# First two expert blocks selected by matrix products, and six blocks moved ahead of a program border

## The chip, the cores and the metric

The kernel runs on one core of a Trainium2 chip, in one launch. The metric is the device time of that core in microseconds (us). A lower time is better.

## The reference

Three transformer layers follow each other on 512 tokens of width 1024, all in float32. The first two have the same form: two kinds of attention, a mixture of experts, and a gated per-layer embedding. The third is of another kind and has no experts. The change touches only the mixture of experts:

```python
g_sel = jnp.argmax(g_logits, axis=-1)                       # one of 4 groups per token
e_prob = jax.nn.softmax(e_logits[rows, g_sel], axis=-1)
top_p, top_i = lax.top_k(e_prob, TOP_K)                     # 2 of the group's 8 experts
gates = g_p[:, None] * top_p / jnp.sum(top_p, axis=-1, keepdims=True)
expert_id = (g_sel[:, None] * EXPERTS_PER_GROUP + top_i).reshape(-1)
...
def expert_block(args):
    xb, e = args
    hid = jax.nn.silu(xb @ w_gate[e]) * (xb @ w_up[e])
    return hid @ w_down[e]
```

There are 32 experts. Each has a gate and an up matrix of 1024 x 256 and a down matrix of 256 x 1024, one megabyte each. Every token goes to two experts, and the two results are added to it with their weights.

## The kernel before, in words

Each of the first two layers has a routing block and an expert block, in the sense of a program block: the program of every engine is cut there, all engines wait for each other at the border, read a value, branch, and go on.

**Routing (`merge_and_route`, L1478).** After the output product of the attention, the tokens x lie in SBUF, 128 per tile in four tiles. TensorE turns x and multiplies it with the router's weights; VectorE finds the two experts of every token and writes `member`, a 0/1 table of tokens by experts. TensorE sums it (L1610, L1612), which gives each token its rank within its expert. From the ranks VectorE works out a slot for each of the 1024 pairs of token and expert, in blocks of 64 slots ("lanes"): block n holds the first 64 tokens of expert n. There are 32 of these, a 33rd for the first overflow, and a rare path (`spilled`) for more. TensorE turns the slots into the token table by L1620 and L1623: for each slot of each block, which token is in it. VectorE stores it as `r.token` and `r.row` (L1779 to L1783). ScalarE meanwhile writes the normed rows of x to DRAM (`xn_rows`, L1654 to L1661). GpSimd then gathers the rows of blocks 0 and 1 (L1561), one indirect transfer for a pair of blocks, into one of two tiles `xs`. This ends the routing block.

**Border.** L1484 waits for all engines, L3325 loads the number of overflow blocks into a register of each engine, and L3143 branches past the rare path.

**Experts (`experts`, L1843).** 33 blocks in order. TensorE's order for block n is: `gate_up(n)` (L1950, 16 products of 64 tokens with 256 columns, each two records in the trace); on even n the turning of the next pair's rows, `turn` (L1939); `down(n - 1)` (L1968); `turn_hidden(n)` (L1959). ScalarE does the silu and evicts the result of `down`; VectorE multiplies silu and up (L2021), copies the turned hidden tile (L2027), and scales the turned rows by the norm's gain (`xsT`, L2012). GpSimd scatters block n's result to DRAM (L1909) and gathers the pair after next (L1902).

**The weights.** Six slots hold the weights of six experts. The routing block's SyncE queue fills all six. In the expert block SyncE goes on with expert 6 in slot 0, and so on (L1885, L1887): gate and up of expert n wait until `gate_up(n - 6)` is done, its down matrix until `down(n - 6)` is done. All three are on one queue, in order:

```python
wait(sp, sem["gu_done"], n - U + 1)
for dst, src in (gate, up):
    sp.dma_start(dst, src).then_inc(w_landed[n % U], 16)
wait(sp, sem["down_done"], n - U + 1)
sp.dma_start(*down).then_inc(down_landed[n % U], 16)
```

The order of all of this is the order in which the code is written; no planner is at work.

Of the kernel before, what the change touches and what calls it, by code (L numbers as in the profile page):

```python
# [1476 lines left out]
def merge_and_route(k, tag, st, attention, second_ready, m, op, r, xn_rows, first, expert_loads, embedding, xs, gathered, done):  # L1477
# [6 lines left out]
    with ExitStack() as ctx:  # L1484
        def sb(name, shape, dt=F32):
# [5 lines left out]
        wide = sb("wide", [P, SPILL * NE])  # L1491
        lgT, ended = wide[:, 0:S // 2], wide[:].rearrange("p (s e) -> p s e", s=SPILL)
# [19 lines left out]
        lane_hot = sb("lane_hot", [P, 8, P], F32R)  # L1512
        block_token = sb("block_token", [P, 8, BLOCKS], F32R)
# [4 lines left out]
                 "gap_ready ratio_done member_ready ranked lane_hot_ready block_token_ready tabled halved cleared token_ready start_ready")  # L1518
        (link_sem, p_turned, gained_ready, turned, out_act, out_dve, logits_done, logits_out, logits_turned, gneg_ready, gexp_done,
         gap_ready, ratio_done, member_ready, ranked, lane_hot_ready, block_token_ready, tabled, halved, cleared, token_ready, start_ready) = sems(  # L1520
# [6 lines left out]
        def _(sp):  # L1527
# [17 lines left out]
            expert_loads.issue(sp, 10)  # L1545

        @block.gpsimd
        def _(pool):
            last_token = pool.to_reg(S - 1)
# [5 lines left out]
            for u in range(GATHERS):  # L1555
                nc.gpsimd.memset(xs[:, u, :], 0.0).then_inc(cleared, 1)
# [3 lines left out]
            for q in range(GATHERS):  # L1560
                nc.gpsimd.indirect_dma_start(out=xs[:, q, :], out_offset=None, in_=xn_rows[:, :],  # L1561
                                             in_offset=bass.IndirectOffsetOnAxis(ap=r.token[:, q:q + 1], axis=0),
                                             bounds_check=last_token, oob_is_err=False).then_inc(gathered[q], 16)

        @block.tensor
        def _(pe):
# [43 lines left out]
            nc.tensor.matmul(k.ps[:, 2, 0:NT * NE], k.neg_before[:], member[:], start=True, stop=False, skip_group_check=True)  # L1610
            for n in range(1, NT + 1):
                last = nc.tensor.matmul(k.ps[:, 2, n * NE:(NT + 1) * NE], k.neg_ones[:], member[:, 0:(NT + 1 - n) * NE],  # L1612
                                        start=False, stop=(n == NT), skip_group_check=True)
            last.then_inc(ranked, 1)

            pe.wait_ge(block_token_ready, 1)
            for i in range(8):
                if i % 4 == 0:
                    pe.wait_ge(lane_hot_ready, 1 + i // 4)
                last = nc.tensor.matmul(k.ps[:, 3, 0:BLOCKS], lane_hot[:, i, :], block_token[:, i, :], start=(i == 0), stop=(i == 7))  # L1620
# [224 lines left out]
def experts(k, ctx, room, tag, r, layer, first, blocks, xn_rows, y_rows, w_gate, w_up, w_down, xs, gathered, opening=None):  # L1845

    nc = k.nc
# [1609 lines left out]
```

## Time and profile before

| what | us |
|---|---|
| median of 3 runs (2473.07 to 2476.53) | 2473.22 |
| the profiled execution | 2474.32 |
| its span in the trace | 2472.4 |
| PE (TensorE) busy | 2280.0 (92%) |
| DVE (VectorE) busy | 993.5 (40%) |
| ACT (ScalarE) busy | 588.0 (24%) |
| POOL (GpSimd) busy | 402.7 (16%) |

402.86 MB go through the core's DMA queues, 372.56 MB of them on the hardware queue q1. The expert stage of the first layer lies at about 464 to 710 us of the span, that of the second at about 1235 to 1485 us.

How to read it: PE is the matmul part of TensorE and PEld its weight load, which runs beside it. A busy share is an average over stages with different limits, so what bounds the expert stage must be read there. "DMA share" is the mean busy share of the 16 DMA engines. A bracket at a row's end tells how long the engine was idle before it, and what ended that. A "q" after an engine's name means its sequencer. `PEclk` is the granted clock of TensorE, 1.00 for 2.4 GHz and 0.50 for 1.2 GHz.

### The profile page before, as it was taken

The numbers are of one execution on the slowest core, as the hardware profiler recorded it, in microseconds if no ns is written. First come the engines' busy times: TensorE is split into PE (matmuls) and PEld (weight loads), VectorE is DVE, ScalarE is ACT, GpSimd is POOL, SyncE is SP. The second block draws the span as 40 slices with busy tenths as digits, with TensorE's granted clock in tenths as the row PEclk, the third lists the DMA queues.
The fourth block names the chain that finished last, engine by engine and source line by source line (L and its number), as shares of the span: only waits on it lengthen the run. The fifth ranks groups of instructions, "written<-read, shape, count | busy, mean of one in ns | idle before, by whom it ended". The sixth has DMA issues, their size and how long they took to land. (4 is left out here: it accounts for less than half of the span.)

```text
span 2472.4 us, 29130 instructions
## 1 busy us (share of the span) xinstructions
PE 2280.0 (92%) x11792; PEld 1688.7 (68%) x11792; DVE 993.5 (40%) x1701; ACT 588.0 (24%) x1213; POOL 402.7 (16%) x399
## 2 busy tenths in 40 slices
PE   7989999689889989999698979899999999999998
PEld 6666788444447767788554446687767887888887
DVE  5545533311135444643411116455653334322234
ACT  3533301211123342410311113323441002100012
POOL 2011111112211101111111212111101211112111
PEclk9999999799989999999899999899999999999999
DMA  5114436699962202234789994332222333233321
GB/s 159 52 53 107 126 109 250 262 415 421 422 272 77 68 26 71 65 94 146 304 337 422 421 373 148 86 86 71 79 69 73 102 104 97 85 99 98 95 102 69
DMA packets 291897, 402.86 MB, mean 163 GB/s; under 512 B 31534, under 2 KB 230958, under 8 KB 273834
## 3 DMA queue, kind: packets, MB, share of 16 engines
q1 hardware_dynamic: 276000, 372.56, 42.1%
q0 software_dynamic: 10176, 16.81, 1.8%
q10 hardware_dynamic: 5578, 11.51, 1.7%
q8 instruction: 98, 1.61, 0.3%
q14 instruction: 45, 0.37, 0.0%
HBM read 388.98 MB, written 30.15 MB: 170 GB/s over the span
## 5 line engine op out<-in xcount | busy, mean ns | idle before, releaser
L138 PE MATMUL banks<-h_split,w_high 128*128 128x512 f32 x2624 | 825.7, 396 | 2.3 <-PEq L3142 1.7
L138 PEld LDWEIGHTS banks<-h_split,w_high 128*128 128x128 f32 x2624 | 480.9, 188 | 104.3 <-issue 8.2
L190 DVE TENSOR_TENSOR w_low<-w_raw,w_high 128x1024 fp32r<-128x1024 f32 (+1 forms) x264 | 316.8, 1201 | 502.3 <-POOL w_high L179 502.2
L179 POOL CAST w_high<-w_raw 128x1024 fp32r<-128x1024 f32 (+1 forms) x264 | 277.0, 1050 | 1458.9 <-PE banks L138 1334.1
L138 PE MATMUL banks<-h_split,w_low 128*128 128x512 f32 x1312 | 512.1, 390 | 0.0
L138 PEld LDWEIGHTS banks<-h_split,w_low 128*128 128x128 f32 x1312 | 246.2, 188 | 52.3
L138 PE MATMUL banks<-w_high,op_split 128*128 128x512 f32 x736 | 228.5, 390 | 1.4 <-DVE mg_part L1355 1.1
L1950 PE MATMUL banks<-expert_ring,ex_xsT 128*64 128x256 f32 x1472 | 181.6, 403 | 21.6 <-DMA expert_ring<-in_w_exp_up 18.6
L1950 PEld LDWEIGHTS banks<-expert_ring,ex_xsT 128*64 128x64 f32 x1472 | 108.0, 145 | 81.1 <-DMA expert_ring<-in_w_exp_up 20.5
L138 PEld LDWEIGHTS banks<-w_high,op_split 128*128 128x128 f32 x736 | 138.1, 188 | 31.9 <-DVE mg_part L1355 2.4
L138 PE MATMUL banks<-w_low,op_split 128*128 128x512 f32 x368 | 143.2, 389 | 0.0
L2021 DVE TENSOR_TENSOR ex_hid<-ex_silu,banks 128x128 f32<-128x128 f32 x66 | 19.0, 288 | 280.2 <-ACT ex_silu L1998 280.2
L1909 POOL DMA_INDIRECT y_rows<-ex_y,route_row x66 | 65.8, 997 | 388.2 <-ACT ex_y L1993 388.2
L138 PE MATMUL banks<-w_high,h_split 128*128 128x512 f32 (+1 forms) x384 | 120.2, 388 | 3.7 <-DVE h_split L361 3.5
L1339 ACT ACTIVATE mg_sig<-banks 128x512 f32<-128x512 f32 x44 | 26.4, 601 | 341.7 <-PE banks L138 341.7
L1968 PE MATMUL banks<-expert_ring,ex_hidT 128*64 128x512 f32 x368 | 90.8, 615 | 0.9 <-issue 0.9
L1939 PE MATMUL banks<-identity,ex_xs 128*128 128x128 f32 x272 | 41.4, 298 | 49.7 <-DMA ex_xs<-xn_rows,route_token 29.6
L138 PE MATMUL banks<-pg_high,h_split 128*128 128x512 f32 x256 | 84.4, 405 | 2.6 <-issue 2.6
L138 PEld LDWEIGHTS banks<-w_high,h_split 128*128 128x128 f32 x384 | 72.9, 195 | 18.6 <-DVE h_split L361 5.1
L1998 ACT ACTIVATE ex_silu<-banks 128x128 f32<-128x128 f32 x66 | 18.3, 278 | 271.7 <-PE banks L1950 271.7
L1950 PE MATMUL banks<-region,ex_xsT 128*64 128x256 f32 x640 | 75.2, 388 | 7.7 <-DMA region<-in_w_exp_up 7.7
L1993 ACT ACTIVATE ex_y<-banks 128x512 f32<-128x512 f32 x66 | 39.4, 597 | 170.7 <-PE banks L1968 170.7
(416 smaller groups left out, 2727.8 us busy)
## 6 DMA issues: line engine op xcount, KB each, us to landing
w_raw<-in_w_in SPq DMA_DIRECT2D x142, 512.0 KB, 4.0
expert_ring<-in_w_exp_gate SPq DMA_DIRECT2D x46, 1024.0 KB
expert_ring<-in_w_exp_up SPq DMA_DIRECT2D x46, 1024.0 KB
expert_ring<-in_w_exp_down SPq DMA_DIRECT2D x46, 1024.0 KB, 22.2
w_raw<-in_w_gu SPq DMA_DIRECT2D x44, 512.0 KB, 4.0
region<-in_w_exp_gate SPq DMA_DIRECT2D x20, 1024.0 KB
region<-in_w_exp_up SPq DMA_DIRECT2D x20, 1024.0 KB
region<-in_w_exp_down SPq DMA_DIRECT2D x20, 1024.0 KB, 17.6
```

The source lines that it names most:

```text
L138: last = nc.tensor.matmul(out, left, right, start=(start and n == 0), stop=(stop and n == 2), skip_group_check=True)
L179: self.nc.gpsimd.tensor_copy(self.high[:, i % self.SPLIT, 0:n], self.raw[:, i % self.RAW, 0:n]).then_inc(self.high_ready, 1)
L190: self.nc.vector.tensor_tensor(self.low[:, i % self.SPLIT, 0:n], self.raw[:, i % self.RAW, 0:n], self.high[:, i % self.SPLIT, 0:n].bitcast ...
L1339: self.nc.scalar.activation(out, gate, ACT.Sigmoid).then_inc(self.sig_done, 1)
L1909: nc.gpsimd.indirect_dma_start(out=y_halves, in_=y[:, n % Y, :], in_offset=None, out_offset=bass.IndirectOffsetOnAxis(ap=r.row[:, at:at + ...
L1939: last = nc.tensor.transpose(k.ps[:, c // 4, (c % 4) * P:(c % 4 + 1) * P], xs[:, q % X, c::DC], k.ident[:])
L1950: last = nc.tensor.matmul(k.ps[LANES * h:LANES * (h + 1), 2 + side, 0:2 * P].rearrange("p (g n) -> p g n", g=2), xsT[:, q % X, c, LANES * ...
L1968: last = nc.tensor.matmul(k.ps[LANES * h:LANES * (h + 1), 5 + n % 2, :], hidT[:, n % 2, LANES * f:LANES * (f + 1)], slots[n % U][1][:, f, ...
L1993: nc.scalar.activation(y[:, n % Y, :], k.ps[:, 5 + n % 2, :], ACT.Copy).then_inc(sem["y_ready"], 1)
L1998: nc.scalar.activation(silu[:, n % 2, :], k.ps[:, 2 + n % 2, 0:P], ACT.Silu).then_inc(sem["silu_done"], 1)
L2021: nc.vector.tensor_tensor(hid[:, n % 2, :], silu[:, n % 2, :], k.ps[:, 2 + n % 2, P:2 * P], ALU.mult).then_inc(sem["hid_ready"], 1)
```

## The change

**Blocks 0 and 1 without a gather.** For each of these two blocks VectorE makes a table `select` of tokens by 64 lanes from the ranks: the norm's factor where the token is in the lane, else 0. TensorE multiplies x with it (`pick`: 8 column groups by 4 tiles, 32 products with a 128x128 stationary tile of x and 64 moving columns). The result is the block's rows, already turned. ScalarE copies it with the gain (`take`, 8 copies of 128x64). `select` lies in the first `xs` tile.

**Six blocks in the routing block.** `gate_up`, `turn_hidden`, `down` and the rest of blocks 0 to 5 now stand in the routing block, before the border, and SyncE issues the loads of experts 6 to 11 there. The token table stands in front of block 0's products. After the border the expert block goes on with block 6. Its first step is to turn the rows of pair 3. The rare path moves to a function of its own, and restores slot 5 and the two gathered pairs.

```diff
+            def pick(b):
+                pe.wait_ge(select_ready, b + 1)
+                for c in range(DC):
+                    for t in range(NT):
+                        last = nc.tensor.matmul(e.pick(b, c), k.x[:, t, c::DC], select[:, b, t, :],
+                                                start=(t == 0), stop=(t == NT - 1))
+                    last.then_inc(e.selected, 1)
+
+            pe.wait_ge(p_taken, 1)
+            pick(0)
             pe.wait_ge(block_token_ready, 1)
...
             last.then_inc(halved, 1)
+            e.gate_up(pe, 0)
+            e.turn_hidden(pe, 0)
+            pick(1)
+            e.gate_up(pe, 1)
+            e.down(pe, 0)
+            e.turn_hidden(pe, 1)
+            e.turn(pe, 1)
+            pe.wait_ge(row_ready, 1)
+            e.down(pe, 1)
+            for n in range(2, EARLY):
+                e.gate_up(pe, n)
+                if n == 2:
+                    e.turn(pe, 2)
+                if n > 2:
+                    e.down(pe, n - 1)
+                e.turn_hidden(pe, n)
+            e.down(pe, EARLY - 1)
...
             expert_loads.issue(sp, 10)
+            for n in range(EXPERT_SLOTS, EXPERT_SLOTS + EARLY):
+                e.load(sp, n)
...
-            for q in range(GATHERS):
-                nc.gpsimd.indirect_dma_start(out=xs[:, q, :], out_offset=None, in_=xn_rows[:, :],
...
+            e.gather(pool, 1, last_token)
+            pool.wait_ge(e.selected, FIRST_PAIR * DC)
+            e.gather(pool, 2, last_token)
+            pool.wait_ge(row_ready, 1)
+            for n in range(EARLY):
+                if n and n % 2 == 0:
+                    pool.wait_ge(e.turned, n // 2)
+                    e.gather(pool, n // 2 + GATHERS, last_token)
+                e.scatter(pool, n, last_row)
...
+            def chosen(b):
+                link(V.tensor_tensor(select[:, b, :, :], lane_next[:].unsqueeze(1).to_broadcast([P, NT, LANES]),
+                                     next_rank[:, :, b:b + 1].to_broadcast([P, NT, LANES]), ALU.is_equal))
+                V.tensor_tensor(select[:, b, :, :], select[:, b, :, :], of_tile(norm.ss[:], LANES), ALU.mult).then_inc(select_ready, 1)
...
+EARLY = 6
...
+    def take(self, act, n):
+        for c in range(DC):
+            act.wait_ge(self.selected, n * DC + self.last_of_bank(n, c) + 1)
+            self.nc.scalar.activation(self.xsT[:, 0, c, LANES * n:LANES * (n + 1)], self.pick(n, c), ACT.Copy,
+                                      scale=self.r.gain[:, c:c + 1]).then_inc(self.taken, 1)
...
     def sync(sp):
-        for n in range(ahead, blocks):
...
+        for n in range(EXPERT_SLOTS + EARLY, e.blocks):
+            e.load(sp, n)
...
-    nc = bacc.Bacc("TRN2", target_bir_lowering=False, num_devices=1)
+    nc = bacc.Bacc("TRN2", target_bir_lowering=False, num_devices=1, dynamic_dma_scratch_size=4096)
```

The order of TensorE from the last rank products to the border, first layer, before:

```order
L1612 MATMUL banks<-rt_member,neg_ones 128x96
L1612 MATMUL banks<-rt_member,neg_ones 128x64
L1612 MATMUL banks<-rt_member,neg_ones 128x32
L1620 MATMUL banks<-rt_block_token,rt_lane_hot 128x48 x8
L1623 MATMUL banks<-rt_block_token,rt_lane_hot 128x48 x4
L1484 UNCONDITIONAL_BRANCH
L3325 TENSOR_LOAD route_spill_expert
L3143 COMPARE_AND_BRANCH
```

And changed (L1632 is `pick`, L2000 `gate_up`, L2009 `turn_hidden`, L2019 `down`, L1984 `turn`):

```order
L1624 MATMUL banks<-rt_member,neg_ones 128x32
L1632 MATMUL banks<-ex_xs,x_tokens 128x64 x32
L1642 MATMUL banks<-rt_block_token,rt_lane_hot 128x48 x8
L1645 MATMUL banks<-rt_block_token,rt_lane_hot 128x48 x4
L2000 MATMUL banks<-expert_ring,ex_xsT 64x256 x16
L2009 MATMUL banks<-identity,ex_hid 128x128
L1632 MATMUL banks<-ex_xs,x_tokens 128x64 x32
L2000 MATMUL banks<-expert_ring,ex_xsT 64x256 x16
L2019 MATMUL banks<-expert_ring,ex_hidT 64x512 x4
L2009 MATMUL banks<-identity,ex_hid 128x128
L1984 MATMUL banks<-identity,ex_xs 128x128 x8
L2019 MATMUL banks<-expert_ring,ex_hidT 64x512 x4
```

The table products (L1620, now L1642) stand behind the 32 products of block 0, and the expert products of six blocks stand before the border, of which the first ones are shown.

SyncE's queue at the same border, before and then changed (the last of the six loads in front of it):

```order
L121 DMA region<-in_w_exp_gate 128x2048
L121 DMA region<-in_w_exp_up 128x2048
L121 DMA region<-in_w_exp_down 128x2x1024
L1484 UNCONDITIONAL_BRANCH
L3325 TENSOR_LOAD route_spill_expert
```

These are the loads of the last slot filled ahead, slot 5. The same place in the changed kernel:

```order
L1949 DMA region<-in_w_exp_down 128x2x1024
L1947 DMA region<-in_w_exp_gate 128x2048
L1947 DMA region<-in_w_exp_up 128x2048
L1949 DMA region<-in_w_exp_down 128x2x1024
L1484 UNCONDITIONAL_BRANCH
L3481 TENSOR_LOAD route_spill_expert
```

The loads of experts 6 to 11 now stand in front of L1484. Those of experts 12 and up stay behind it.

VectorE behind the rank products, before and then changed:

```order
L1740 TENSOR_SCALAR rt_gneg<-rt_gtop 128x4
L1741 TENSOR_TENSOR rt_gap<-rt_etop 128x4
L1746 TENSOR_TENSOR rt_beyond<-banks,rt_neg_base 128x224
L1748 TENSOR_REDUCE rt_spills<-rt_beyond 128x32
L1749 TENSOR_TENSOR rt_slotv<-rt_base,banks 128x128
```

The token table's first step follows at once on two small ones. The same place in the changed kernel:

```order
L1789 TENSOR_TENSOR rt_gap<-rt_etop 128x4
L1800 SCALAR_TENSOR_TENSOR rt_next_rank<-banks,rt_member 128x8
L1796 TENSOR_TENSOR ex_xs<-rt_lane_next,rt_next_rank 128x256
L1798 TENSOR_TENSOR ex_xs<-ex_xs,route_ss 128x256
L1805 TENSOR_TENSOR rt_beyond<-banks,rt_neg_base 128x224
L1807 TENSOR_REDUCE rt_spills<-rt_beyond 128x32
```

Three instructions for block 0's `select` (the tile `ex_xs`) now stand ahead of the first step of the token table, `rt_beyond`.

## Rows read from the trace of the kernel before

**Rows 1.** Stretches of 5 us; columns as their head line says.
```profile
core 0: us, PE busy (x) PEld busy (x) DVE busy (x) ACT busy (x) POOL busy (x), PEclk, DMA share, GB/s
445.00:450.00 5.00, 0.05 (x1) 0.00 (x0) 4.57 (x16) 2.42 (x10) 0.00 (x0) 0.51 0.70 241
...
460.00:465.00 5.00, 0.53 (x3) 0.54 (x4) 0.00 (x0) 1.28 (x1) 0.00 (x0) 0.50 0.03 8
...
470.00:475.00 5.00, 5.00 (x35) 3.30 (x33) 0.38 (x2) 0.28 (x1) 0.00 (x0) 0.76 0.11 20
...
485.00:490.00 5.00, 5.00 (x38) 2.51 (x38) 1.58 (x3) 0.60 (x1) 1.66 (x2) 1.00 1.01 420
```

**Rows 2.** Timeline of SyncE's queue: start us, duration us, then the transfer.
```profile
473.83 0.34 SPq L1885 DMA_DIRECT2D expert_ring<-in_w_exp_gate  x1
...
480.35 0.38 SPq L1887 DMA_DIRECT2D expert_ring<-in_w_exp_down  x1
```

**Rows 3.** Timeline of TensorE, first layer's expert blocks, same columns.
```profile
464.47 1.97 PE L1939 MATMUL banks<-identity,ex_xs 128*128 128x128 f32 x8 [10.43 <-issue]
467.91 5.89 PE L1950 MATMUL banks<-expert_ring,ex_xsT 128*64 128x256 f32 x32 [1.47 <-DVE ex_xsT L2012]
...
474.71 0.27 PE L1959 MATMUL banks<-identity,ex_hid 128*128 128x128 f32 x1
...
480.50 3.67 PE L1950 MATMUL banks<-expert_ring,ex_xsT 128*64 128x256 f32 x32
...
487.31 3.67 PE L1950 MATMUL banks<-expert_ring,ex_xsT 128*64 128x256 f32 x32
490.81 1.89 PE L1968 MATMUL banks<-expert_ring,ex_hidT 128*64 128x512 f32 x8
...
492.88 3.67 PE L1950 MATMUL banks<-region,ex_xsT 128*64 128x256 f32 x32
...
509.52 3.67 PE L1950 MATMUL banks<-expert_ring,ex_xsT 128*64 128x256 f32 x32
...
700.33 5.36 PE L1950 MATMUL banks<-expert_ring,ex_xsT 128*64 128x256 f32 x32 [1.85 <-DMA expert_ring<-in_w_exp_up]
```

**Rows 4.** Timeline of VectorE in the routing.
```profile
443.46 0.43 DVE L1736 TENSOR_TENSOR rt_onehot<-route_iota,rt_esel 128x256 f32<-128x256 f32 x1
...
445.09 0.39 DVE L1746 TENSOR_TENSOR rt_beyond<-banks,rt_neg_base 128x224 f32<-128x224 f32 x1 [0.50 <-PE banks L1612]
```

**Rows 5.** Timeline of TensorE: slot table at 451 us, another product at 262 us.
```profile
262.28 1.16 PE L1053 MATMUL banks<-da_v,da_diffT 128*128 128x128 f32 x8
...
451.27 1.91 PE L1620 MATMUL banks<-rt_block_token,rt_lane_hot 128*128 128x48 f32 x8 [6.22 <-DVE rt_block_token L1771]
```

**Rows 6.** The lines that end a program block: durations ns min/median/max.
```profile
L1484 POOLq DRAIN  x2: 4837/5104/5372, 454.8 to 1226.5; - x2
...
L3142 POOLq DRAIN  x2: 5055/5105/5155, 904.5 to 1713.0; - x2
...
L3325 PEldq TENSOR_LOAD <-route_spill_expert x2: 310/396/483, 460.5 to 1231.6; - x2
...
L3143 PEldq COMPARE_BRANCH  x2: 3312/3330/3348, 461.1 to 1232.0; - x2
```

**Rows 7.** Timeline of GpSimd and ScalarE: gather, scatter, eviction.
```profile
456.09 1.01 POOL L1561 DMA_INDIRECT ex_xs<-xn_rows,route_token  x1 [0.31 <-issue]
...
481.23 1.02 POOL L1909 DMA_INDIRECT y_rows<-ex_y,route_row  x1 [13.53 <-ACT ex_y L1993]
...
480.35 0.60 ACT L1993 ACTIVATE ex_y<-banks 128x512 f32<-128x512 f32 x1 [1.44 <-PE banks L1968]
```

**Rows 8.** DMA of 454 to 475 us, of 455 to 725, of 462 to 463.
```profile
ex_xs<-xn_rows,route_token POOLq DMA_INDIRECT x3, 4.0
...
ex_xs<-xn_rows,route_token POOLq DMA_INDIRECT x17, 8.2
...
q8 instruction: 1, 0.02, 6.2%
```

More of the change, by code:

```diff
@@ L1667, in _ @@
             nc.scalar.activation(gap[:], gap[:], ACT.Exp).then_inc(ratio_done, 1)
+            act.preload_act_table_set("silu_and_others")
+            e.take(act, 0)
+            e.silu(act, 0)
+            e.take(act, 1)
+            for n in range(1, EARLY):
+                e.silu(act, n)
+                e.evict(act, n - 1)
+            e.evict(act, EARLY - 1)
         @block.vector
@@ L1793, in _ @@
             link(V.tensor_tensor(r.gate[:, 1, :], r.gate[:, 0, :], gap[:], ALU.mult))
+            e.hidden(dve, 1)
+            e.hidden_turned(dve, 1)
+            e.weigh(dve, 1)
+            for n in range(2, EARLY):
+                e.hidden(dve, n)
+                if n == 2:
+                    e.weigh(dve, 2)
+                e.hidden_turned(dve, n)
 EXPERT_WORDS = DC * 2 * HID + 2 * D
@@ new lines, in gpsimd @@
+        e.pooled(pool, EARLY, last_token, last_row)
+        pool.wait_ge(e.down_done, e.blocks)
+        gate_stream.split_highs(pool, 0, gate_stream.SPLIT)
+    def tensor(pe):
+        e.multiply(pe, EARLY)
+        pe.wait_ge(w_landed[0], 16)
+        pe.wait_ge(w_landed[1], 16)
+        for i in range(NT):
+            wait(pe, embedding.ready, i - 1)
+            embedding.product(i, k.ps[:, i % 2, :]).then_inc(multiplied, 1)
+    def scalar(act):
+        e.activate(act, EARLY)
+        for i in range(NT):
+            act.wait_ge(multiplied, i + 1)
+            embedding.take(i, k.ps[:, i % 2, :])
@@ L3312, in first_layer @@
                                        for n, part in (("gu", slice(0, 2)), ("down", slice(2, 3)))))
-        gathered = sems(k, ending, " ".join(f"ex_gathered{u}" for u in range(GATHERS)))
+        tiles = (xs, *(k.room(room, "ex_" + n, shape) for n, shape in (
+            ("xsT", [P, GATHERS, DC, P]), ("silu", [P, 2, P]), ("hid", [P, 2, P]), ("hidT", [P, 2, P]), ("y", [P, OUTPUTS, 512]))))
+        e = Experts(k, ending, "ex", tiles, r, i, 0, ALWAYS, 1, xn_rows, y_rows, weights, expert_loads)
         results = Rows(k, ending, "cb", y_rows)
@@ L3326, in first_layer @@
         with nc.If(spilled > ALWAYS - EXPERTS), ExitStack() as rest, nc.Block() as block:
-            more = experts(k, rest, rest, "sp", r, i, EXPERTS, SPILL, xn_rows, y_rows, *weights, xs, gathered)
+            more = spilled_experts(k, rest, "sp", e, tiles, r, i, xn_rows, y_rows, weights)
             block.sync(more[0])
@@ L3332, in first_layer @@
             block.vector(more[4])
-        moe = experts(k, ending, room, "ex", r, i, 0, ALWAYS, xn_rows, y_rows, *weights, xs, gathered,
-                      (expert_loads, embedding, results, gate_stream, ended))
+        moe = remaining_experts(k, ending, "ex", e, embedding, results, gate_stream, ended)
         k.used_sems -= ended
```

430 lines of the change are left out of this document (242 added, 188 removed).

## The prediction

> **What bounds the kernel now.** I read the page first, then the stretches of 5 us, SyncE's queue, TensorE's timeline, and last the border. The page's chain stays on TensorE and says nothing of the experts, so the stage has to be read by itself. The weights' stream sets its end. In [rows 1] the DMA engines are full at 420 GB/s from about 475 us on, and TensorE's last `gate_up` waits for its up matrix until 700.33 [rows 3]. Ahead of the stream there is a hole: at 460 to 465 us the engines move 8 GB/s [rows 1], since the six slots are full and expert 6 may only be loaded once `gate_up(0)` is done. SyncE issues it at 473.83 [rows 2]. So what counts is neither when block 0 starts nor how busy TensorE is. It is how much DMA time stands empty before the stream runs for good.
>
> The stream's price: from 473.83 to 700.33 come 27 experts less one down matrix, 80 matrices. That is 226.5 us, 2.83 us each. The bubble ahead of expert 6's down matrix (issued at 480.35) is 0.9 of this, so I take 2.8 us a matrix, 8.4 a block, gathers and scatters included. A block costs TensorE 5.57 us without a `turn` (487.31 to 492.88) and 6.81 with one (480.50 to 487.31) [rows 3]. It is faster than its weights.
>
> **Routing, first layer.** VectorE has the ranks at 445.09. Before the token table it now makes `select`: one small instruction and two of 128x256 at 0.43 us [rows 4], about 1.15 us with the gaps. `pick(0)` starts at 446.25 and needs no gather.
>
> Its 32 products are 64 records, as each full float32 product is two in the trace. No row shows this shape. Eight records of 128x128 stationary and 128 moving columns took 1.16 us, (1.16 - 0.27) / 7 = 0.13 us each at the high clock, and other groups of this line 0.11; eight of 48 columns at the low clock took 1.91, or 0.22 each [rows 5]. I take 0.12 and 0.22. A `pick` costs 7.7 us at 2.4 GHz and 14 at 1.2, and these are its bounds. The granted clock is 0.51 at 445 to 450 us [rows 1], so `pick(0)` starts low. Before, TensorE began at 464.47 and again at 467.91 after a short stop, and the mean of 0.76 over 470 to 475 us puts the rise at 472.4: 7.9 or 4.5 us of work. I take 5: 23 records low, 41 high, 10 us, end at 456.2 (457.6 with 7.9).
>
> The twelve table products are ready at about 452.5 but queue behind `pick(0)`: 1.4 us, to 457.6. ScalarE's copies lie beside them. `gate_up(0)` takes 3.67, to 461.3. Before it was done at 473.8, so it is **12.5 us earlier**, and expert 6's gate and up are issued then.
>
> **What the next blocks give back.** `turn_hidden(0)` waits for silu and product, 0.9 us after `gate_up` as at 474.71 [rows 3], to 462.4. Then `pick(1)` 7.7, to 470.1; `gate_up(1)` to 473.6; `down(0)` to 475.4, which was done at 480.31. Then `turn_hidden(1)` 0.3, `turn(1)` 1.2, `down(1)` 1.8: `gate_up(2)` starts at 478.7, where it was 480.50. Of 12.5 us 1.8 are left, as `pick(1)` and the once idle first microseconds fill up with work. With 5.0 (6.81 less the `down` already done), 5.57 and 5.57, blocks 3, 4, 5 start at 483.7, 489.3, 494.8. `down(5)` ends at 502.8, and no gather is waited for, as pair 2's is asked for at 470.
>
> **The border.** It was crossed in the idle hole and now stands between blocks 5 and 6. GpSimd's drain comes last: its last gather was issued by 457.10 [rows 7], and the drain ended at 454.8 + 5.37 = 460.2. Load and branch follow, with 3.3 us of branch on TensorE [rows 6], which starts at 464.47: 7.4 us from GpSimd's last issue. Ahead of that now stand `evict(5)` and its scatter: from eviction to the scatter's end 1.9 us (480.35 to 482.25) [rows 7]. So TensorE starts at 502.8 + 9.3 = 512.1. What followed before, turning, scaling, and `gate_up` at the low clock of 5.89 us, took 464.47 to 473.8, 9.3 us. It follows again, after 9 us of rest: `gate_up(6)` is done at 521.4, where it was 509.52 + 3.67 = 513.2.
>
> **The queue.** Expert 6's gate and up run 461.3 to 466.9; then the queue is empty until `down(0)` at 475.4. From there 16 matrices are asked for in time (expert 6's down and experts 7 to 11): 16 x 2.8 = 44.8, to 520.2. Expert 12 may be issued at 521.4: 1.2 us empty. Its gate and up end at 527.0; its down waits for `down(6)`, 521.4 + 1.2 + 0.3 + 3.5 + 1.8 = 528.2. Before, the same matrix started at 480.35 + 18 x 2.8 = 530.75. The stream after it is the same, so **2.6 us are gained in a layer**, not 12.5.
>
> **The price not shown.** The border was crossed with empty queues and will be crossed with full ones. A gather takes 4.0 us to land with empty queues and 8.2 with full ones [rows 8]. The branch includes one fetch of instructions, the single packet at 462 us [rows 8]; at full queues it costs 0 to 4.2 us more. The drain ended about as the gather landed, 456.09 + 4.0 = 460.1, so it may wait for the scatter's landing: 0 to 4.2 more. Against that, the drain of another block (L3142) takes 5.1 us with no gather in sight [rows 6]. A fetch is one packet where a gather is over a hundred. I take 1.5 us for both together, nearest to the low end. Nothing cheaper than empty queues is possible.
>
> The Trainium skill, page "Runtime: NRT & Kernel Launch", section "Instruction fetch mechanics", says a taken branch whose target isn't in the engine's window must fetch it by DMA before going on. The 3.3 us agree, and it speaks against moving the border into the full stream. Its page "DMA: Bandwidth & Descriptors", section "Queues, rings and completion order", says that an engine takes turns between queues packet by packet. By that rule the fetch would wait for a packet or so, and the sum would be near 2.6 us a layer; by the gather's row it would be up to 4.2 us worse.
>
> **Sum.** Per layer -2.6 + 1.5 = -1.1. The second layer shows the same steps (drain, load, branch within 0.6 us in the x2 rows of [rows 6]). Twice that is -2.2 on the profiled execution's own 2474.32, which is 2472.1. The median of the runs is 1.1 lower, so 2471. The rest costs nothing: silu's table load moves to where ScalarE rests, the rare path's tables lie behind block 0's hidden tile in VectorE's slack, and fewer bytes are gathered.
>
> **Rivals.**
> 1. *The gain of block 0 is carried through*: 2 x 12.5 = 25 us, 2448. For it: the hole is real. Against: expert 6's down matrix waits for `down(0)`, which gains only 4.9 us, and TensorE reaches block 6 8 us later than before. 5%.
> 2. *The queue never runs dry at the border.* If TensorE's chain is 1.2 us or more shorter, expert 12 starts at 520.2 and the gain reaches at most 530.75 - 525.8 = 5.0 a layer: 2463. For it: the clock may rise after 4 us, a border may be quicker. 22%.
> 3. *The border under full queues*, slower. It decides from 2.6 us extra on, since the queue is dry by then and each further microsecond goes to the end. With the drain's 4.2 and the 1.5, -2.6 + 5.7 = +3.1 a layer, 2479.4; with both whole, +5.8, 2485. 18%.
> 4. *The clock stays low through `pick(0)`*: 14 for 10 us, +4 on everything behind, +2.9 a layer, 2479; with `pick(1)` low too +9 a layer, 2491. For it: 7.9 us passed before. Against: `pick` is unbroken work. 12%.
> 5. *The descriptor space does not do*: each of GpSimd's transfers waits for the one before. Three a pair of blocks at 8.2 are 24.6 us against 16.8 of weights, 7.8 x 13 x 2 = +203 us. For it: a quarter of the space. Against: at most three are in flight. 5%, with other mishaps.
>
> My forecast keeps 38%. A measurement tells about 0.2%, 5 us, from no change. Faster by more: rivals 1 and 2 and a little, 29%. Slower: 3 to 5 less a little, 34%. Within: 37%. The range of 2462 to 2486 holds cases 2 and 3 whole; it leaves out 1, 5, and the far end of 4. The likeliest case's own range is 2468 to 2475.
>
> **What would show it.** After the change: expert 6 issued at about 461 and its down at about 475; `pick` of 10 and 7.7 us; TensorE's rest at the border about 9 us; a dip in the DMA engines of 1 to 3 us just before expert 12; TensorE's last `gate_up` still waiting for weights, at 699. I am wrong if the branch or the drain is much longer than 3.3 and 5 us, if there is no dip, or if the last blocks no longer wait for weights.

## The result and the profile after

The changed kernel takes 2520.11 us (median of 4 runs, 2517.44 to 2524.7), the kernel before 2474.7 beside it. The ratio is 1.0185, with a 95% interval of 1.0167 to 1.0203: **slower by 45 us**, outside the range of 2462 to 2486. The profiled execution took 2517.44 us, with a span of 2515.6.

TensorE's timeline in the first layer answers [rows 3] and [rows 5]; columns are start, duration, the group, and the idle time before it.

```profile
446.76 15.47 PE L1632 MATMUL banks<-ex_xs,x_tokens 128*128 128x64 f32 x64 [1.27 <-DVE ex_xs L1798]
461.99 1.88 PE L1642 MATMUL banks<-rt_block_token,rt_lane_hot 128*128 128x48 f32 x8
...
464.65 5.28 PE L2000 MATMUL banks<-expert_ring,ex_xsT 128*64 128x256 f32 x32
...
470.80 15.38 PE L1632 MATMUL banks<-ex_xs,x_tokens 128*128 128x64 f32 x64
486.11 4.79 PE L2000 MATMUL banks<-expert_ring,ex_xsT 128*64 128x256 f32 x32
...
517.46 1.94 PE L2019 MATMUL banks<-region,ex_hidT 128*64 128x512 f32 x8 [0.43 <-issue]
534.58 1.94 PE L1984 MATMUL banks<-identity,ex_xs 128*128 128x128 f32 x8 [15.19 <-issue]
...
732.98 1.94 PE L2019 MATMUL banks<-expert_ring,ex_hidT 128*64 128x512 f32 x8 [0.43 <-issue]
```

`pick(0)` starts within half a microsecond of the forecast and takes 15.5 us instead of 10. `pick(1)`, the next group of L1632, holds TensorE from 470.80 until `gate_up(1)` starts at 486.11: 15.3 us instead of 7.7. At the border TensorE rests 15.19 us, not 9.3 (10.8 with the 1.5 us that the forecast added for full queues). The stage's last `down` ends at 734.92. Before, it ended at 710.04 (the row of 708.10, 1.94 us long).

SyncE's queue, in answer to [rows 2]: gate of expert 6, its down matrix, gate of expert 12.

```profile
469.97 0.33 SPq L1947 DMA_DIRECT2D expert_ring<-in_w_exp_gate  x1
...
492.66 0.38 SPq L1949 DMA_DIRECT2D expert_ring<-in_w_exp_down  x1
...
544.15 0.34 SPq L1947 DMA_DIRECT2D expert_ring<-in_w_exp_gate  x1
```

The forecast had 461.3, 475.4 and 521.4. The stretches of 5 us, with the columns of [rows 1], show what the clock and the DMA engines did meanwhile.

```profile
455.00:460.00 5.00, 5.00 (x23) 5.00 (x22) 0.00 (x0) 0.68 (x3) 0.00 (x0) 0.50 0.16 66
460.00:465.00 5.00, 5.00 (x24) 4.90 (x25) 0.57 (x3) 0.52 (x2) 0.00 (x0) 0.50 0.01 3
...
470.00:475.00 5.00, 4.37 (x19) 4.37 (x20) 2.93 (x11) 0.26 (x1) 0.00 (x0) 0.98 0.83 293
475.00:480.00 5.00, 5.00 (x22) 5.00 (x23) 0.00 (x0) 0.72 (x3) 0.00 (x0) 0.50 0.30 126
...
540.00:545.00 5.00, 5.00 (x32) 3.31 (x29) 0.29 (x1) 0.28 (x1) 0.00 (x0) 0.70 0.02 9
```

Two things are to be seen. In a pick the weight load (PEld) is busy all the time, and a record takes 0.23 us at a granted clock of 0.98 (4.37 us for 19) as at 0.50 (5.00 us for 22). And TensorE was granted 0.50 all through `pick(0)`, 0.98 at the start of `pick(1)`, and 0.50 again inside it. At 540 to 545 us the DMA engines move 9 GB/s: the queue is dry before expert 12, for some 5 us and not for one.

The border's instructions, in answer to [rows 6] (durations in ns, min/median/max):

```profile
L1484 POOLq DRAIN  x2: 7257/7411/7565, 520.1 to 1315.0; - x2
...
L3298 PEldq COMPARE_BRANCH  x2: 5908/6175/6442, 528.5 to 1323.0; - x2
```

### The profile page after: what moved, and what is told of

It reads as the page before. It is cut to its first block and busy times, and to the rows that moved or that the text cites. A ratio compares the mean times of both kernels' runs of the same rounds, so it can differ in the third digit from the quotient of the medians.

```text
span 2515.6 us, 29654 instructions
## 1 busy us (share of the span) xinstructions
PE 2337.7 (93%) x12032; PEld 1747.4 (69%) x12032; DVE 993.9 (40%) x1709; ACT 595.6 (24%) x1245; POOL 400.0 (16%) x397
## 5 line engine op out<-in xcount | busy, mean ns | idle before, releaser
L2000 PE MATMUL banks<-expert_ring,ex_xsT 128*64 128x256 f32 x1472 | 182.3, 404 | 4.7 <-issue 2.9
L2000 PEld LDWEIGHTS banks<-expert_ring,ex_xsT 128*64 128x64 f32 x1472 | 108.7, 145 | 65.1 <-issue 15.9
L1984 PE MATMUL banks<-identity,ex_xs 128*128 128x128 f32 x256 | 40.3, 305 | 67.5 <-DMA ex_xs<-xn_rows,route_token 37.1
L2019 PE MATMUL banks<-expert_ring,ex_hidT 128*64 128x512 f32 x368 | 92.1, 623 | 0.9 <-issue 0.9
L1984 PEld LDWEIGHTS banks<-identity,ex_xs 128*128 128x128 f32 x256 | 33.2, 195 | 81.5 <-DMA ex_xs<-xn_rows,route_token 47.0
```

The source lines that it names most:

```text
L1984: last = self.nc.tensor.transpose(self.k.ps[:, c // 4, (c % 4) * P:(c % 4 + 1) * P], self.xs[:, q % GATHERS, c::DC], self.k.ident[:])
L2000: last = self.nc.tensor.matmul(self.k.ps[LANES * h:LANES * (h + 1), 2 + side, 0:2 * P].rearrange("p (g n) -> p g n", g=2), self.xsT[:, q % ...
L2019: last = self.nc.tensor.matmul(self.k.ps[LANES * h:LANES * (h + 1), 5 + n % 2, :], self.hidT[:, n % 2, LANES * f:LANES * (f + 1)], self.sl ...
```

## The experiments

The opening of the program shifts by up to 2 us from run to run (the rank products start between 443.0 and 446.2 us, in the kernel before at 444.3), so that times of different runs are compared as distances within the stage where it matters. Each median is best set against that of the kernel before beside it, which lies between 2472.0 and 2474.7 us.

**1. `scratch_only`: the kernel before, with the smaller descriptor space alone.**

```diff
-    nc = bacc.Bacc("TRN2", target_bir_lowering=False, num_devices=1)
+    nc = bacc.Bacc("TRN2", target_bir_lowering=False, num_devices=1, dynamic_dma_scratch_size=4096)
```

> The kernel before, with only the descriptor space of GpSimd's transfers cut from 16384 to 4096 bytes a partition. If the loss of 45 us comes from the picks and the border (my theory now), this is the time of the kernel before, 2474 within 4 us, and the gathers land in 8 us in the expert stage as before. If the smaller space makes an indirect transfer wait for the one before it, the expert stages are longer, up to the whole 45 us, with GpSimd's issues no longer 1.0 us.

Measured 2473.28 us, ratio 1.0013 [0.9984, 1.0042]. The smaller space costs nothing that can be measured, and a gather between 540 and 700 us still takes 8.3 us to land (median). Rival 5 falls. One thing differs in its trace: the drain of the other block (L3142), 5.1 us in [rows 6], is 3.1 us here.

**2. `gather_six`: six blocks ahead of the border, but blocks 0 and 1 gathered as before.**

```diff
-            e.gather(pool, 1, last_token)
-            pool.wait_ge(e.selected, FIRST_PAIR * DC)
-            e.gather(pool, 2, last_token)
+            e.gather(pool, 0, last_token)
+            e.gather(pool, 1, last_token)
...
-            pick(0)
...
+            e.turn(pe, 0)
             e.gate_up(pe, 0)
+            e.turn(pe, 1)
             e.turn_hidden(pe, 0)
-            pick(1)
             e.gate_up(pe, 1)
             e.down(pe, 0)
             e.turn_hidden(pe, 1)
-            e.turn(pe, 1)
...
```

> The changed kernel with blocks 0 and 1 gathered as before (no select, no pick, the token table alone on TensorE), but still six blocks ahead of the border and the small descriptor space. Theory 'picks at the low clock': without 2 x 15.3 us of picks the chain is short; the first turn starts at about 459 (5 us earlier than before), expert 6 is issued at 468, expert 12 at about 524, and the whole is 2471 (2466 to 2478). Theory 'border under full queues': TensorE's rest at the border stays 15 us and carries most of the loss, so this is still slower than the kernel before by 15 us or more, 2490 to 2510.

Measured 2477.37 us, ratio 1.0028 [1.0014, 1.0041]. That is 4.8 us above the kernel before beside it, so that the picks account for some 41 of the 45 us. The time is at the upper end of the first theory's range; the border kept its length as the second had it, without carrying most of the loss. Expert 6 is asked for at 467.05, since block 0 no longer has the border ahead of it (473.83 in [rows 2]), and expert 12 at 524.32. The border is long here too. TensorE's restart, and the two instructions:

```profile
514.88 1.94 PE L1975 MATMUL banks<-identity,ex_xs 128*128 128x128 f32 x8 [14.91 <-issue]
```

```profile
L1484 POOLq DRAIN  x2: 6941/7082/7222, 500.6 to 1272.2; - x2
...
L3289 PEldq COMPARE_BRANCH  x2: 6238/6243/6248, 508.5 to 1280.1; - x2
```

So moving the border alone gains about 6 us ahead of block 0 (6.8 by the clock time, of which 0.7 is this run's earlier opening) and gives them back behind block 5, and a little more.

**3. `border_after_two`: the changed kernel with its border behind block 1.**

```diff
-            e.turn(pe, 1)
             pe.wait_ge(row_ready, 1)
-            e.down(pe, 1)
...
-EARLY = 6
+EARLY = 2
```

> The changed kernel with two blocks ahead of the border in place of six; the picks stay. The border is then crossed with little in the queues. If full queues make the border long, TensorE's rest there falls from 17 us to about 10 and its branch from 6 us to 3.3; but expert 8 must wait behind the border (issued at about 514 in place of 499), so the whole is about 5 us slower than the changed kernel, 2525 (2518 to 2532). If the border costs 15 us whatever the queues hold, expert 8 comes at 520 and the whole is 2540. If the border's place in the stream were the loss, and not the picks, this would be near 2480.

Measured 2529.9 us, ratio 1.0233 [1.0215, 1.025]. The time is in the expected range, the account of it is not right: the rest was to be about 10 us, and expert 8, asked for at 521.18, was to come at 514. TensorE's restart in both layers and its second weight load in the first, then the drain and the branch:

```profile
511.80 1.87 PE L1981 MATMUL banks<-identity,ex_xs 128*128 128x128 f32 x8 [16.00 <-issue]
511.81 1.46 PEld L1981 LDWEIGHTS banks<-identity,ex_xs 128*128 128x128 f32 x7 [3.05 <-issue]
...
1310.36 1.94 PE L1981 MATMUL banks<-identity,ex_xs 128*128 128x128 f32 x8 [12.46 <-issue]
```

```profile
L1484 POOLq DRAIN  x2: 7427/7444/7462, 496.5 to 1298.6; - x2
...
L3295 PEldq COMPARE_BRANCH  x2: 3462/3562/3661, 504.8 to 1306.7; - x2
```

The drain takes 7.4 us, but the branch only 3.5. The DMA engines are full (410 GB/s) when the drain begins at 496.5 and nearly still (share 0.18) at 505 to 510, when the branch runs. The long drain and the long branch can come apart. The rest is 12.46 us in the second layer. In the first it is 16.00, since TensorE stops for another 3.05 us behind its first weight load. The profile names nothing that it waits for there; `one_pick` has a stop of 3.66 us between its first transposes, also in the first layer only. No run shows what these stops are.

**4. `one_pick`: one pick for both blocks, 128 moving columns in place of twice 64.**

```diff
-                        last = nc.tensor.matmul(e.pick(b, c), k.x[:, t, c::DC], select[:, b, t, :],
+                        last = nc.tensor.matmul(e.pick(c), k.x[:, t, c::DC], select[:, :, t, :],
...
-            pick(1)
```

> The changed kernel with one pick for both blocks: 32 products with 128 moving columns in place of 2 x 32 with 64, and nothing else moved (block 1's select is made before the token table, 0.9 us). Theory 'picks': one of two picks of 15.3 us is gone, 14 us a layer, 2491 if the clock stays low in it; if the wider products raise the granted clock, the pick takes 8 to 11 us in place of 15.5 and the whole is about 2480. Theory 'border': the rest at the border stays 15 to 17 us and the gain is less than 10 us, above 2505.

Measured 2482.63 us, ratio 1.0045 [1.0031, 1.0059]. That is 10.0 us above the kernel before beside it, so half the records bring about 35 of the 45 us back. The expected 2480 was for a pick of 8 to 11 us at a rising clock. The clock did rise, but the pick did not get shorter:

```profile
447.64 15.53 PE L1632 MATMUL banks<-ex_xs,x_tokens 128*128 128x128 f32 x64 [2.06 <-DVE ex_xs L1796]
```

```profile
450.00:455.00 5.00, 5.00 (x23) 5.00 (x23) 4.00 (x15) 0.00 (x0) 0.00 (x0) 0.82 1.00 418
455.00:460.00 5.00, 5.00 (x23) 5.00 (x23) 0.00 (x0) 1.14 (x4) 0.00 (x0) 1.00 0.23 92
```

64 records take 15.5 us again, with twice the columns and at a granted clock of 0.82 and 1.00. What the clock gave back lies behind the pick: the table products and both first `gate_up` run at 1.00 and take 4.0 us less than in the changed kernel (1.2, 1.6 and 1.1), beside the 15.3 of the pick that is gone. Neither the columns nor the clock set the price of a record. The weight load does: it is busy in 5.00 of 5.00 us, and one LDWEIGHTS takes 336 ns in the median:

```profile
L1632 PEld LDWEIGHTS banks<-ex_xs,x_tokens x128: 312/336/338, 447.6 to 1239.8; 128*128 128x128 f32 x128
```

The load's tile is `k.x[:, t, c::DC]`, every eighth float32 of a row, 32 bytes apart.

**5. `pick_contiguous`: the same two picks from neighbouring columns.**

```diff
-                        last = nc.tensor.matmul(e.pick(b, c), k.x[:, t, c::DC], select[:, b, t, :],
+                        last = nc.tensor.matmul(e.pick(b, c), k.x[:, t, c * P:(c + 1) * P], select[:, b, t, :],
```

> The changed kernel, but the pick's stationary tile takes 128 neighbouring columns of the stream, k.x[:, t, c*P:(c+1)*P], where it took every eighth one, k.x[:, t, c::DC]. It leaves the columns of the first two blocks' rows in another order, so their results are not the reference's; the number and size of all instructions stay. Theory A (the pick is bound by its weight load, and the load is slow because its columns lie 32 bytes apart): the LDWEIGHTS of the pick fall from 335 ns to about 195 ns (the 193 ns of the transposes), a record from 0.24 us to about 0.12 us at full clock, each pick from 15.4 to 7.7 us if the clock is high and 13 to 14 us if it stays at half; with both at full clock gate_up(0) is done at about 461 and the time falls by 2 layers x (2 x 7.6) = 30 us to about 2490. Theory B (the load is slow whatever its columns are, or the clock alone makes the pick long): LDWEIGHTS stay at 335 ns, the picks at 15.4 us, and the time at 2520.

This kernel leaves out the right order of the columns for blocks 0 and 1, so its results are not the reference's, and only its times count. Measured 2495.4 us, ratio 1.0102 [1.0056, 1.0148]: some 23 us faster than the changed kernel, each against the kernel before beside it, with four runs from 2490.0 to 2511.9. Both picks, and the weight loads of the second alone:

```profile
446.87 13.89 PE L1632 MATMUL banks<-ex_xs,x_tokens 128*128 128x64 f32 x64 [1.26 <-DVE ex_xs L1798]
...
469.88 7.26 PE L1632 MATMUL banks<-ex_xs,x_tokens 128*128 128x64 f32 x64
```

```profile
L1632 PEld LDWEIGHTS banks<-ex_xs,x_tokens x64: 192/192/246, 469.7 to 476.8; 128*128 128x128 f32 x64
```

At the high clock the load falls from 336 to 192 ns and the pick to 7.26 us, close to the 7.7 of the forecast. At the low clock (0.50 up to 460 us) it is 333 ns and the pick 13.89 us, the forecast's 14. The forecast's two prices, 0.12 and 0.22 us a record, were those of a contiguous tile; the strided one costs 0.24 at either clock. So the stride costs 8.1 us of a pick at the high clock, and only 1.6 at the low one. The clock also behaves otherwise: it is 1.00 through the whole second pick, where the strided pick lost it. Yet it stays low through `pick(0)`, where `one_pick` was given 0.82 at 450 to 455 us.

**6. `select_stationary`: operands changed over, on the frame of `gather_six`.** The selection of both blocks (128 lanes, contiguous) is loaded, the tokens are what moves, 512 columns at a time.

```diff
-                for c in range(DC):
+                for half in (1, 0):
                     for t in range(NT):
-                        last = nc.tensor.matmul(e.pick(b, c), k.x[:, t, c::DC], select[:, b, t, :],
+                        last = nc.tensor.matmul(k.ps[:, half, :], chosen_rows[:, t, :], k.x[:, t, half * 512:(half + 1) * 512],
```

> The variant that gathers and has six blocks ahead of the border, but with the rows of the first two blocks made by products with the operands changed over: the selection of both blocks is the stationary tile (128 lanes, contiguous), the stream is what moves (512 columns), 8 products in all, 16 records; the result is a pair of rows as a gather would leave it, and goes through the same transposes. Theory A (a product's price is its weight load where it moves few columns, and its columns where it moves 512): 16 records of 0.43 us = 7 us at half clock, 3.5 us at full clock, from about 447 to 454, in place of 30.8 us; the eviction and 8 transposes follow, gate_up(0) is done at about 463 (467.05 with the gather), expert 12 is asked for at about 520.5 (524.3), and the time is 2 x 3.5 us under that variant's 2477: 2470, about the kernel before. Theory B (something else in the first two blocks' products holds TensorE): gate_up(0) done at 470 or later and the time at 2483 or more.

Measured 2469.98 us, ratio 0.9993 [0.9982, 1.0004]: the same idea at no loss. The total is the expected one, the pick is not. It was to take 7 us at most and takes 9.5, since a record takes 0.59 us and not 0.43; `gate_up(0)` is done within a microsecond of the expected time all the same.

```profile
446.85 9.47 PE L1631 MATMUL banks<-x_tokens,ex_xs 128*128 128x512 f32 x16 [2.06 <-DVE ex_xs L1796]
...
460.03 3.67 PE L2003 MATMUL banks<-expert_ring,ex_xsT 128*64 128x256 f32 x32 [1.47 <-DVE ex_xsT L2065]
...
511.20 1.94 PE L1987 MATMUL banks<-identity,ex_xs 128*128 128x128 f32 x8 [14.57 <-issue]
```

16 records do both blocks in 9.5 us; the changed kernel takes 128 in 30.8. `gate_up(0)` then runs at the high clock and is done at 463.7. Experiment 9 tries whether the 14.57 us at the border are what keeps this version from being faster.

**7. `border_dry_queues`: `gather_six` with only experts 6 and 7 asked for ahead of the border**, so that the weight queue is dry there.

```diff
-            for n in range(EXPERT_SLOTS, EXPERT_SLOTS + EARLY):
+            for n in range(EXPERT_SLOTS, EXPERT_SLOTS + AHEAD):
...
+AHEAD = 2
```

> The variant that gathers all blocks and has six of them ahead of the border, with only experts 6 and 7 asked for there (before: six), so that the weight queue has run dry well before GpSimd's last scatter at about 500. Theory A (TensorE's branch and GpSimd's drain are long because the weight queues are full): the branch falls from 6.2 to 3.3 us and the drain after the last issue from 7.1 to about 5 us, so the rest of TensorE at the border from 14.9 to about 9 to 10 us. Theory B (the border's cost comes from its place, behind scatters and a long stretch of TensorE work): 6.2 and 7 us stay, the rest stays at about 15 us. Either way the time rises, since experts 8 to 11 are fetched later: estimate 2490 to 2515.

One run, 2499.33 us; the border is what it was made for. TensorE's restart, and GpSimd's drain:

```profile
512.47 1.94 PE L1976 MATMUL banks<-identity,ex_xs 128*128 128x128 f32 x8 [8.58 <-issue]
```

```profile
L1484 POOLq DRAIN  x2: 3058/3068/3079, 504.6 to 1287.0; - x2
...
L3290 PEldq COMPARE_BRANCH  x2: 3474/3631/3788, 508.5 to 1290.7; - x2
```

With 29 to 70 GB/s on the DMA engines from 500 to 510 us, the drain is 3.1 us, where 5 were expected, the branch 3.6 and the rest 8.6. TensorE and GpSimd do the same work up to this border as in `gather_six`. So full queues cost 4.0 us in the drain and 2.6 in the branch (6.3 us by the rests).

**8. `border_scatter_landed`: `gather_six` with GpSimd waiting for its scatters' landing before the drain.**

```diff
+            for u in range(OUTPUTS):
+                pool.wait_ge(e.scattered[u], 16 * len(range(u, EARLY, OUTPUTS)))
```

> The variant that gathers all blocks and has six of them ahead of the border, with GpSimd waiting for the landing of its own scatters before it goes into the border. Theory A (GpSimd's drain of 7.1 us is the wait for the scatter to land): the wait takes some 5 us, the drain behind it under 1 us, and the rest of TensorE at the border stays at 14.9 us; time 2477. Theory B (the drain costs a fixed time after the landing as well): the drain keeps 3 us or more behind the wait, and the rest grows by 2 to 4 us per layer; time 2480 to 2485.

One run, 2491.45 us.

```profile
L1484 POOLq DRAIN  x2: 943/950/957, 509.1 to 1280.4; - x2
```

The drain behind the wait is 0.95 us, so nearly all of its 7.1 us is the landing. The rest is 16.49 us, 1.6 more than in `gather_six`, between the two theories. The first layer's stage ends at 712.7, in `gather_six` at 712.3. The 14 us of the total arise in the second layer's stage, in its waits for gathers: 49.2 us of them from 500 to 1500 us, against 33.1 in `gather_six`. Why they are longer in this one run isn't shown; `gather_six` itself has four of its ten runs at 2482.8 to 2485.7 and six below 2479.

**9. `scatters_behind`: `select_stationary` with the last three scatters and a gather behind the border.** The rare path gets an output buffer of its own for this.

```diff
-            for n in range(EARLY):
+            for n in range(SCATTERED_EARLY):
                 if n % 2 == 0:
                     pool.wait_ge(e.turned, n // 2 + 1)
                     e.gather(pool, n // 2 + GATHERS, last_token)
                 e.scatter(pool, n, last_row)
...
+SCATTERED_EARLY = 3
...
-        e.pooled(pool, EARLY, last_token, last_row)
+        e.pooled(pool, SCATTERED_EARLY, last_token, last_row)
```

> The variant select_stationary, but GpSimd issues only the scatters of blocks 0 to 2 and the gathers up to the fourth pair ahead of the border; the scatters of blocks 3 to 5 and the next gather are its first work behind it. Theory A (the border's rest is GpSimd's last landing plus the branch, one behind the other): GpSimd has been still since about 484 and its landings are over when TensorE has emptied its queue at 496.7, so the barrier stands at about 497.5 (504.4 in select_stationary), the branch still takes about 6 us, TensorE restarts at about 504.5 (511.2), expert 12 is asked for at about 514.2 (520.9), before the queue runs dry at about 516.5, so some 5.5 us of the 6.7 are kept per layer: about 2459. Theory B (the drain takes its 7 us under full queues whatever was issued before, or the branch lengthens to fill the time): the restart stays at 509 or later and the time at 2468 to 2470.

Measured **2456.89 us, ratio 0.9939 [0.9923, 0.9955]**: 15 us faster than the kernel before, and the fastest version tried.

```profile
496.60 1.94 PE L2023 MATMUL banks<-region,ex_hidT 128*64 128x512 f32 x8 [0.43 <-issue]
506.07 1.94 PE L1988 MATMUL banks<-identity,ex_xs 128*128 128x128 f32 x8 [7.53 <-issue]
```

```profile
L1484 POOLq DRAIN  x2: 6668/6829/6990, 485.4 to 1246.5; - x2
...
L3291 PEldq COMPARE_BRANCH  x2: 5822/5900/5978, 500.1 to 1260.9; - x2
```

```profile
510.00:515.00 5.00, 5.00 (x28) 3.16 (x26) 0.00 (x0) 0.00 (x0) 0.00 (x0) 0.53 1.02 417
515.00:520.00 5.00, 5.00 (x47) 3.38 (x44) 1.78 (x4) 0.28 (x1) 0.00 (x0) 1.00 1.00 406
```

The drain still takes 6.8 us, but beside TensorE's work: it starts at 485.4. The branch keeps its 5.9 us. The rest is 7.5 in place of 14.6 us, expert 12 is asked for at 515.72, and the DMA engines stay full through 520 us, with one dip to 331 GB/s at 520 to 525. That is rival 2 of the forecast, nearly: the queue is not dry before expert 12.

**10. `after_scatters_behind`: the same move in the changed kernel itself**, with both picks as they are. The diff is that of 9.

> The changed kernel, with both picks as they are, but the scatters of blocks 3 to 5 and the gather that stood with block 4 issued by GpSimd behind the border. Theory A (the border's two terms are independent of the picks and go one behind the other into the end): TensorE's rest between the last down product of block 5 and the first transpose falls from 15.2 to about 7.5 us as it did with select_stationary, expert 12 is asked for at about 536.5 (544.15), before the queue runs dry at about 539, and 5.5 to 7 us per layer reach the end: 2506 to 2509. Theory B (the loss in the changed kernel is all in the picks, and a shorter border only meets a wait for weights or gathers): 2517 or more.

Measured 2507.4 us, ratio 1.0127 [1.0102, 1.0152], inside what theory A gave.

```profile
529.26 1.94 PE L1985 MATMUL banks<-identity,ex_xs 128*128 128x128 f32 x8 [7.86 <-issue]
```

TensorE rests 7.86 us, where it rested 15.19, and expert 12 is asked for at 539.09, 2.6 us later than expected, 1.9 of which are this run's later opening. Issuing the last scatters and the gather behind the border is thus worth roughly the same with the picks as without: 10 to 14 us over both layers here, by which time or ratio one takes, and 13 from experiment 6 to 9. The four runs spread from 2497.6 to 2514.1, so this size is rough.

**11. `gathers_behind`: the kernel before, its border where it was, the first two gathers issued behind it.**

```diff
-            for q in range(GATHERS):
-                nc.gpsimd.indirect_dma_start(out=xs[:, q, :], out_offset=None, in_=xn_rows[:, :],
...
+        for u in range(X):
+            gather(u, first // 2 + u, gathered)
```

> The kernel before, with its border where it was, but the first two gathers issued behind it. Theory A (the drain of 5 us there is the landing of these gathers): TensorE's branch starts at about 457.5 in place of 461.1 and ends at 460.8, beside the gathers, which are issued at 457.6 and 459.1 and land about 4.0 us after; the first transposes start at about 462 to 463 (464.47), and the time falls by 2 layers x 1.5 to 2.4 us, to 2468 to 2470. Theory B (the drain takes its time without a transfer too, or the gather lands later beside the branch): no change, 2471 to 2475.

Measured 2470.68 us, ratio 0.999 [0.9981, 0.9999]. The time is between the two theories. GpSimd's drain falls from 5.1 to 0.04 us and the branch begins at 456.9, not at 461.1 [rows 6]:

```profile
L1484 POOLq DRAIN  x2: 34/37/40, 453.1 to 1223.6; - x2
...
L3135 PEldq COMPARE_BRANCH  x2: 3312/3500/3688, 456.9 to 1227.3; - x2
```

```profile
462.17 1.97 PE L1931 MATMUL banks<-identity,ex_xs 128*128 128x128 f32 x8 [9.03 <-DMA ex_xs<-xn_rows,route_token]
```

The first transposes start 2.3 us earlier than in [rows 3], of which 0.9 is this run's earlier opening. TensorE rests 9.03 us where it rested 10.43, now waiting for the gather: 1.4 us gained in this layer. The median gains 1.6 us in all. So in the kernel before, too, the drain was the gathers' landing, one behind the other with the branch.

## Why the prediction was wrong

**Routing and `pick(0)`.** `select` and the start were right (446.25 forecast, 446.76 measured). The step that failed is the price of a record, "0.12 and 0.22" and with it "a `pick` costs 7.7 us at 2.4 GHz and 14 at 1.2, and these are its bounds". The rows it came from load other tiles, and I applied them to a tile read at a stride of 32 bytes without asking what the stride costs. The picks took 15.47 and 15.3 us, or 0.24 us a record. Experiment 5 shows both halves: the stride makes it 0.24 at the high clock (7.26 us for the pick without it), and the low clock costs `pick(0)` 13.9 us even without it.

The Trainium skill, page "Advanced Engine Details and Errata", section "Memory Cachelines", says SBUF is read in lines of 16 bytes and wants at least two hits in a line for full speed. A stride of 32 bytes has one hit a line, so by that rule the load is slow. Experiments 4 and 5 agree at the high clock: 336 ns against 192. At the low clock the contiguous load takes 333 ns, and the stride hardly shows. The rule was at hand, and I didn't weigh it.

**The clock.** "I take 5" us until it rises inside `pick(0)` was wrong: the granted clock is 0.50 from 445 to 465 us, and it falls again within `pick(1)`. That is rival 4, which I gave 12%, with "`pick` is unbroken work" against it. TensorE did work without a break there, and the clock stayed low all the same. Why it does is not shown. It rose at 450 to 455 us in `one_pick` (granted 0.82 there) and in `select_stationary` (0.84), and stayed at 0.50 until 465 us with this `pick(0)`, strided or contiguous. The products behind a pick pay as well: the table and `gate_up(0)` took 1.3 and 1.6 us more than forecast, `gate_up(1)` 1.1.

**The border.** "TensorE starts at 502.8 + 9.3" failed by 5.9 us: the rest was 15.2. The mechanism was named, and the 1.5 us taken for it was too small. In the changed kernel drain and branch are 7.4 and 6.2 us, where they were 5.1 and 3.3. Experiment 7 puts 4.0 and 2.6 us of that on the full queues, 6.6 of bounds that went to 8.4 together. I had let another block's drain of 5.1 us without a gather [rows 6], and the branch's single packet, talk me towards the low end. That other drain is no measure of this one: only a cast of GpSimd stands beside it in the traces. Its median is 5.1 and 5.3 us in the two kernels with the default descriptor space and 2.4 to 3.1 in all others, for a reason that no run shows. Rival 3 happened, at 18%.

**The sum.** Against the forecast's own times, expert 12 comes 22.75 us late: 8.4 us up to the start of `pick(1)`, 7.6 more in it, 1.1 in `gate_up(1)`, half a microsecond less in the blocks between, 5.9 at the border, and 0.3 behind it. Its down matrix, which began at 530.75 by the forecast's count of the stream before, is issued at 550.66, and the layer's last matrix at 699.29, where it was 678.87. So for the stream the step on the queue held: what comes late behind a dry queue stays late.

The stage did not follow the stream alone. The first ends 24.9 us later, the second 44.1 in all (1528.6 against 1484.5). The 5 us that the stream doesn't account for are TensorE's own. These are its waits from block 6 to the end of the first stage (us in total, times, longest; without the border's), in the kernel before from 509.5 us and then in the changed one from 535:

```profile
PE banks L1939 <- DMA ex_xs<-xn_rows,route_token: 13.1, 10, 2.3
PE banks L1950 <- DMA expert_ring<-in_w_exp_up: 8.1, 4, 2.7
PE banks L1950 <- DMA region<-in_w_exp_up: 2.8, 2, 2.1
...
PE banks L1984 <- DMA ex_xs<-xn_rows,route_token: 20.1, 11, 3.4
```

Before, TensorE waits 24.0 us, 10.9 of them for weights. Changed, it waits 20.1, all for gathers, and from the start of `gate_up(6)` to the end of the stage it needs 197.0 us (537.95 to 734.92) where it needed 200.5 (509.52 to 710.04). So at the end of the first layer no `gate_up` waits for weights any more, which the forecast had wrong; in the second layer the last one still does, for 1.9 us. The forecast gave TensorE 12.4 us for a pair of blocks (5.57 and 6.81) against 16.8 of weights, and put its waits for gathers at nothing. With them a pair takes it 14.6 us, so that after a late start it is the limit and not the stream. A gather between 540 and 700 us takes 9.3 us to land (median), where it took 8.3; why stays open.

**The rivals.** I told rivals 3 and 4 as alternatives, and both came true, on top of a price outside its bounds. No case held two of them, so the range ended at 2486. Rival 1 was excluded for the right reason: `select_stationary` has `gate_up(0)` done at 463.7, 10 us earlier than before, and the time is the same. Rival 2 allowed a gain of 5.0 us a layer at most for a queue that never runs dry; experiment 9, with other picks, gains 15.3 in both layers, more than that bound. Rival 5 fell with experiment 1.

## What to carry to other kernels

Price a product by its weight load first: look at how the stationary tile is read (a stride of 32 bytes cost 336 ns instead of 192) and how few columns move per load; here changing the operands over turned 128 records into 16. Ask too which engine becomes the limit once the chain is late, waits for gathers included. A program border moved into a busy stretch pays for every transfer that GpSimd still has in flight there, so issue the last ones behind it. And where several rivals can be true together, give that case a time and a chance too.

## What was unexpected of the hardware

- The branch that took 3.3 to 3.9 us with idle DMA engines (the kernel before, experiments 1 and 11) took 5.8 to 6.5 under a full weight queue (eight kernels), and 3.5 to 3.8 wherever the queue was dry at that moment (experiments 3 and 7), whatever the border's place.
- GpSimd's drain at this border is the landing of its indirect transfers: 0.04 us with none in flight, 0.95 behind an explicit wait, 3.1 (a scatter) to 5.5 (gathers) with dry or idle queues, 6.7 to 7.8 with full ones.
- With a strided stationary tile TensorE had the same speed at a granted clock of 0.50 and of 1.00. In the changed kernel it also lost the high clock within the second pick, where `pick_contiguous` kept it; `one_pick`, strided too, kept it. What makes the difference isn't shown.
